# Spatial gating unit: mixing products placed between the z tiles, channel tiles finished one at a time, silu ahead of the slab halves

## The reference, cut to what matters

```python
def sgu_branch(h, w_in, ln_g, ln_b, w_s, b_s, w_out):
    uv, z = jnp.split(h @ w_in, [2 * SGU_WIDTH], axis=-1)
    u, v = jnp.split(jax.nn.gelu(uv), 2, axis=-1)
    v = layernorm(v, ln_g, ln_b).reshape(bsz, L // SGU_CHUNK, SGU_CHUNK, SGU_GROUPS, SGU_GROUP_DIM)
    w = jnp.where(tril[None], w_s, 0.0)
    s = jnp.einsum('gts,bnsgc->bntgc', w, v) + b_s.T[:, :, None]
    return (u * s.reshape(bsz, L, SGU_WIDTH) * jax.nn.silu(z)) @ w_out
```

## Time and profile before

| | us |
|---|---|
| median of 3 runs | 2149.76 (2148.75 to 2155.48) |
| profiled execution, its own time | 2146.33 |
| span of its trace, first to last instruction | 2144.4 |
| busy in the span: PE / DVE / ACT / POOL | 1979.3 / 1328.9 / 856.7 / 465.2 |
| mean granted clock of PE | 0.972 |

### The profile page before, as it was taken

The page is one execution under the profiler, slowest core; times in us unless marked ns, Lnnn a source line. Parts: engine busy times, 40 slices in busy tenths (PEclk is TensorE's granted clock), DMA queues, the critical chain, the costliest instruction groups (busy, mean ns, idle before and its releaser), DMA issues.

```text
span 2144.4 us, 24860 instructions
## 1 busy us (share of the span) xinstructions
PE 1979.3 (92%) x9910; PEld 1555.9 (73%) x9910; DVE 1328.9 (62%) x1920; ACT 856.7 (40%) x1236; POOL 465.2 (22%) x393
## 2 busy tenths in 40 slices
PE   4999898999999999999998899989989999899986
PEld 3777776788567888768897776867777766578865
DVE  5998985726549235544566454677378477637474
ACT  3325656312278224422332343355352354434332
POOL 5871110404159403032400101011002010100001
PEclk9999999999999999999999999999999999999998
DMA  3334431234222534433556626211132210123211
GB/s 131 120 145 142 139 125 54 81 120 148 103 98 84 171 118 157 158 95 131 186 147 149 149 80 125 79 59 41 62 112 83 84 40 20 40 79 129 97 60 59
DMA packets 63747, 225.21 MB, mean 105 GB/s; under 512 B 14144, under 2 KB 31216, under 8 KB 43280
## 3 DMA queue, kind: packets, MB, share of 16 engines
q1 hardware_dynamic: 22896, 162.54, 21.2%
q0 software_dynamic: 19760, 45.83, 7.2%
q10 hardware_dynamic: 20976, 15.26, 3.3%
HBM read 208.72 MB, written 14.81 MB: 104 GB/s over the span
## 4 chain that ended last, share of the span: by engine, by line
PE 64%; DVE 11%; ACT 5%; issue 3%; ACTq 1%; DMA 0%; POOL 0%; DVEq 0%; POOLq 0%
PE bank L486 18%; PE bank L487 18%; PE bank L488 18%; PE bank L485 2%; DVE ring_low L448 2%; PE bank L3362 1%; ACT ring_high L443 1%; PE bank L3393 1%; ACTq L2537 1%; ACT swa_s L3254 1%; PE bank L2061 1%; PE bank L622 1%; DVE lru_x L1975 1%; DVE swa_s L3172 1%; PE bank L3378 1%
## 5 line engine op out<-in xcount | busy, mean ns | idle before, releaser
L486 PE MATMUL bank<-h_high,ring_high 128*128 128x512 f32 x1248 | 504.7, 404 | 37.2 <-DVE h_low L1454 12.1
L448 DVE TENSOR_TENSOR ring_low<-ring,ring_high 128x2048 fp32r<-128x2048 f32 x136 | 326.5, 2401 | 316.4 <-ACT ring_high L443 316.1
L487 PE MATMUL bank<-h_low,ring_high 128*128 128x512 f32 x1248 | 491.9, 394 | 0.0
L488 PE MATMUL bank<-h_high,ring_low 128*128 128x512 f32 x1248 | 491.2, 394 | 0.0
L443 ACT ACTIVATE ring_high<-ring 128x2048 fp32r<-128x2048 f32 x145 | 277.4, 1913 | 475.1 <-PE bank L488 472.4
L486 PEld LDWEIGHTS bank<-h_high,ring_high 128*128 128x128 f32 x1248 | 238.1, 191 | 104.3 <-issue 35.7
L487 PEld LDWEIGHTS bank<-h_low,ring_high 128*128 128x128 f32 x1248 | 238.2, 191 | 52.8 <-issue 4.4
L488 PEld LDWEIGHTS bank<-h_high,ring_low 128*128 128x128 f32 x1248 | 238.0, 191 | 51.1
L448 POOL TENSOR_TENSOR ring_low<-ring,ring_high 128x2048 fp32r<-128x2048 f32 x9 | 44.1, 4904 | 375.6 <-ACT ring_high L443 375.6
L486 PE MATMUL bank<-gated_high,ring_high 128*128 128x512 f32 x256 | 104.8, 409 | 8.2 <-DVE sq L3658 5.0
L487 PE MATMUL bank<-gated_low,ring_high 128*128 128x512 f32 x256 | 102.6, 401 | 0.0
(11 more groups left out here) (520 smaller groups left out, 3833.8 us busy)
## 6 DMA issues: line engine op xcount, KB each, us to landing
ring<-slabs SPq DMA_DIRECT2D x149, 1024.0 KB, 4.8
acs_rows<-acs_rows POOLq DMA_DIRECT2D x16, 512.0 KB, 5.3
s_outputs<-s_ca POOLq DMA_DIRECT2D x4, 1152.0 KB, 5.0
x<-xT SPq DMA_DIRECT2D x2, 2048.0 KB, 8.7
exp_acs<-acs_rows POOLq DMA_DIRECT2D x16, 256.0 KB, 9.6
s_b<-s_br POOLq DMA_DIRECT2D x8, 512.0 KB, 4.6
s_rows<-s_powers POOLq DMA_DIRECT2D x16, 256.0 KB, 6.5
s_inputs<-s_w POOLq DMA_DIRECT2D x8, 512.0 KB, 3.0
```

Source lines behind the costliest of these rows:

```text
L448: dve.tensor_tensor(self.ring_low[:, s % RING, :], self.ring[:, s % RING, :], self.ring_high[:, self.splits_before[s] % AHEAD, :].bitcast( ...
L486: pe.matmul(out, w[0], x[0], start=start, stop=False)
L487: pe.matmul(out, w[0], x[1], start=False, stop=False)
L488: return pe.matmul(out, w[1], x[0], start=False, stop=stop)
```

## The change

A table `mixed` says which channel tiles' mixing goes behind which z tile: 0 behind z tile 4, 1 and 2 behind 5, 3 and 4 behind 6, and 5 to 7 behind 7. On PE the mixing products of those channel tiles stand right behind the z tile's products. On DVE the bias, the product with u and the gated low half of the tile before are in a function `mix(j)`, called behind the same z tiles; the low half of a slab moves behind `times_root` and `factor(i - 1)`, and the mask moves from i = 4 to i = 3, behind V's last token tile. On ACT silu of a tile comes ahead of the slab's high half, and the gated high halves are spread likewise. No instruction's size changes.

```diff
+    mixed = {4: (0,), 5: (1, 2), 6: (3, 4), 7: (5, 6, 7)}
...
         @block.scalar
...
             for i, (u, _) in enumerate(tiles):
-                C.split_high(act, u)
                 C.read(act, u)
                 act.activation(L.Z[:, i, :], L.Z[:, i, :], ACT.Silu).then_inc(gate.curve.sem, 1)
-            for j in range(KD):
-                gate.high_on_act(act, j)
+                C.split_high(act, u)
+                for j in mixed.get(i, ()):
+                    gate.high_on_act(act, j)
...
         @block.vector
...
-                if i == TC:
+                if i == TC - 1:
                     dve.tensor_tensor(L.W[:], L.W[:], C.mask[:].unsqueeze(1).to_broadcast([P, 16, P]), ALU.mult)\
                         .then_inc(wm.sem, 1)
-                C.split_low(dve, u)
                 C.full(dve, u)
                 times_root(dve, i, C.bank[u.b]).then_inc(C.bank_read[u.b], 1)
                 if i > 0:
                     factor(i - 1)
-            factor(KD - 1)
-            for j, u in enumerate(banks):
+                C.split_low(dve, u)
+                for j in mixed.get(i, ()):
+                    if j == KD - 1:
+                        factor(j)
+                    mix(j)
...
         @block.tensor
...
-            for t in tiles:
+            for i, t in enumerate(tiles):
                 C.gemm(pe, t, C.H.tiles(KD), seen)
-            pe.wait_ge(wm.sem, wm.at(0))
-            for j, u in enumerate(banks):
-                C.open(pe, u)
-                for n in range(TC):
+                for j in mixed.get(i, ()):
+                    u = banks[j]
+                    C.open(pe, u)
                     if j == 0:
-                        pe.wait_ge(vn.sem, vn.at(n))
+                        pe.wait_ge(wm.sem, wm.at(0))
+                        pe.wait_ge(vn.sem, vn.at(TC - 1))
```

More of the change, by code:

```diff
@@ L3625, in factor, with mix @@
                 dve.tensor_tensor(L.U[:, i, :], L.U[:, i, :], L.Z[:, i, :], ALU.mult).then_inc(gate.factor.sem, 1)
+            def mix(j):
+                u = banks[j]
+                C.full(dve, u)
+                v = lambda ap: ap.rearrange("p (n t) -> p n t", n=TC)
+                b = L.BS[:, j, :].unsqueeze(1).to_broadcast([P, TC, P])
+                s = C.sq[:, j % 4, :]
+                if j >= 4:
+                    dve.wait_ge(gate.mul.sem, gate.mul.at(j - 4))
+                dve.tensor_tensor(v(s), v(C.bank[u.b][:]), b, ALU.add).then_inc(C.bank_read[u.b], 1)
+                C.read(dve, u)
+                dve.wait_ge(gate.factor.sem, gate.factor.at(j))
+                dve.tensor_tensor(L.U[:, j, :], L.U[:, j, :], s, ALU.mult).then_inc(gate.mul.sem, 1)
+                if j > 0:
+                    gate.low_on_dve(dve, j - 1)
             for t in range(TC):
@@ L3668, in _ @@
             seen = set()
-            for t in tiles:
+            for i, t in enumerate(tiles):
                 C.gemm(pe, t, C.H.tiles(KD), seen)
-            pe.wait_ge(wm.sem, wm.at(0))
-            for j, u in enumerate(banks):
-                C.open(pe, u)
-                for n in range(TC):
+                for j in mixed.get(i, ()):
+                    u = banks[j]
+                    C.open(pe, u)
                     if j == 0:
-                        pe.wait_ge(vn.sem, vn.at(n))
[L3677 to L3681, removed]
+                        pe.wait_ge(wm.sem, wm.at(0))
+                        pe.wait_ge(vn.sem, vn.at(TC - 1))
+                    for n in range(TC):
+                        for e in range(2):
+                            g = 2 * j + e
+                            mm = pe.matmul(C.bank[u.b][64 * e:64 * e + 64, n * P:(n + 1) * P], L.V[:, n, g * 64:g * 64 + 64],
+                                           L.W[:, g, :], start=True, stop=True)
+                    mm.then_inc(C.bank_full[u.b], 1)
 def branch_sgu(C, last):
```

## The result

| | us |
|---|---|
| before, median of 12 runs | 2149.45 (2146.08 to 2155.48) |
| after, median of 12 runs | 2153.41 (2150.53 to 2157.75) |
| ratio after / before | 1.0018, 95% interval 1.0010 to 1.0025 |
| profiled execution of after: its span, clock | 2151.6, 0.972 |

The change costs 4.0 us (0.18%), with an interval that excludes zero. The two spans differ by more, 7.2 us, so I cut them at two marks: V's first normalising instruction, and the first product of the output projection.

What follows compares the result with a forecast made beforehand. The prediction took DVE's steps up to channel tile 6's bias addition as the bound. Waits of +3.8 plus clock and late tiles of +1.0 gave +4.8 us, so 2154.5 on the median of 2149.76, range 2149 to 2160.

Steps and rivals of the forecast that it cites:

- Bound: The output's first product waits for DVE's bias addition of channel tile 6, ending 2076.70, 0.36 us ahead of PE.
- the walk along DVE's steps: DVE's steps timed one by one to channel tile 6's addition, ending 2080.35 against 2076.70 before: +3.65 us.
- Two new waits: DVE waits 2.0 us for ACT's high half also behind z tiles 1 and 3: +4.0 us, less 0.2.
- Stall A: PE idle before z tile 4, whose slab's low half comes late: it starts 3.2 us later.
- Stall B: PE idle before mixing tile 0, between z tiles 4 and 5, waiting for the masked weights: 4.4 us.
- The clock and late tiles: Half clock after PE's idle stretches brings DVE z tile 5 late (+0.7) and tile 7 late (+0.3): together +1.0 us.
- The row of steps: DVE's steps ahead of channel tile 6's addition stay the same before and after; only waits change.
- PE becomes the bound: Rival: half clock through mixing tile 0 and z tile 5 (10.9 us) on PE; +9.4 us, 2159.2, chance 0.20.
- No cost: Rival: ACT's order costs DVE nothing, PE still waits for the mask; about +0.5 us, 2150.3, chance 0.13.
- a gain: Rival: mixing fills DVE's two earlier waits and the output starts at full clock; -6.0 us, 2143.8, chance 0.05.

Runs made afterwards that it cites:

- The square: Four variants of the changed kernel, between the marks: mixing 0 behind z tile 5, slab order before 49.00, changed 52.98 us; behind tile 4, 53.68 and 54.43.
- The run with neither cost: Changed kernel with slab halves in the order of before and channel tile 0's mixing behind z tile 5: 49.00 us between the marks, ratio 1.0001.
- the rearranged kernel: Changed kernel with mask in the stage ahead, high half ahead of silu, last slab's halves at the end, mixing from z tile 5: 2138.97 us, ratio 0.9946.

## Why the prediction was right, and where not

**Bound.** Right for the end, and too short. After the change too the bias addition of channel tile 6 releases the output's first product, 0.35 us ahead of it. But the earlier trace rows begin one row too late: ahead of ACT's high half stands the last product of z tile 7 (2058.63, shown above). DVE's row of steps alone set the end only from there. That PE's tile 7 came last before the change shows in the rows too: that wait was 2.10 us where the others are 1.9, and ACT started 0.19 us after its silu had ended (2058.17 plus 0.53). The margin was so small that the walk along DVE's steps gave nearly the same times, and so this slip did not spoil the forecast.

**Two new waits, +4.0 less 0.2.** Right in place and size: four waits of 1.90 where 2.0 were forecast and 1.91 and 2.10 stood before. The square gives 3.98 for the order, with the stall on the mask taken out. With the stall in, the waits behind tiles 3 and 5 are no longer on the chain, which goes from the mask on DVE over PE's mixing and z tiles 5 to 7.

**Stall A, 3.2.** Measured 3.13. **Stall B, 4.4 at full clock, 2.8 with tile 4 at half clock** (the mask at 2049.65 less 2046.9). Measured 2.55, with low clock behind A. That is under the 3 to 4.4 which the prediction gave as its sign, and its own figure with the low clock was under it as well.

**The clock and late tiles, +1.0.** Right in kind, short in size. DVE waits 0.57 for tile 5 and 0.72 for tile 7, and taking stall B away gave back 1.45. Tile 5 was expected at +0.7 and tile 7 at +0.3.

**The row of steps.** One slip, the other way. The prediction has the steps ahead of channel tile 6's addition the same before and after, and the walk put factor 7 ahead of channel tile 5's addition. In the changed code it stands behind the addition of channel tile 6 (the row at 2085.57 behind the one at 2083.64). Before, it stood ahead of all mixing on DVE:

```profile
2063.65 1.48 DVE L3625 TENSOR_TENSOR sgu_u<-sgu_u,sgu_z 128x512 f32<-128x512 f32 x2
```

These are factors 6 and 7. They took 1.39 us until the next instruction (2065.04) and not 1.20, because factor 7 waited for silu of tile 7. So 0.79 us leave the path, for which the prediction has no term. The run with neither cost shows it: 49.00 against 49.99, of which 0.79 is the factor and 0.21 the shorter last wait.

**Sum.** Forecast +4.8. Counted on DVE's rows: 3.59 more waiting for ACT, 1.29 for PE, 0.79 less for the factor, and 0.32 because an instruction with a wait behind it takes its full 0.68 and not the 0.60 after which the next one starts otherwise (four times more than before). That is +4.41, the stretch is +4.44, and the runs' medians differ by +3.96. The end of the span takes 0.43 back, nearly all of it (0.40) in the first nine products of the output, where the low clock ends sooner than before; I had called that 1.5 either way. On the median I forecast 2154.5, between 2149 and 2160, and it is 2153.4. That it came so near is partly luck: the late tiles were 0.45 short and the factor of 0.79 had no term, and the two go opposite ways.

**The rivals.** *PE becomes the bound* did not come about at its size: tile 5 at half clock took from 2053.98 until DVE had it at 2061.20, 7.2 us, and not 10.9. The low clock ended within it (0.74 in 2056 to 2058, 1.00 after). But its mechanism is nearer than its number says: the chain does run over PE from the mask to tile 7, and with ACT's order undone DVE waits 3.85 and 1.97 for PE. *No cost* would need both costs away (49.00); its sum has a slip, since 2077.5 less 2076.7 is +0.8 and not +0.5. The reason that I gave against a gain, that the mixing stands behind the low halves in DVE's order and fills no wait, fits the rows: all four waits stayed. In the rearranged kernel channels 0 and 1 stand ahead of the low half, and it waits for nothing.

**What the prediction had wrong underneath.** Its +1.0 is what the late tiles add on top of a DVE that is already late, and as such it is right in kind. What it does not see is that the stall alone would cost nearly as much as the whole change. Had I been asked what the change costs without its new order, I would have said +1.8 (that is the expectation on record) and it was +3.7. The step that I left out is that the high half behind a z tile needs the end of that tile on PE, so whatever delays PE comes to DVE by way of ACT. The same tie is why moving the mask alone gave nothing, where a row of steps on DVE alone would give 2.2.

The Trainium skill's rule that I weighed against the change ("TensorE: Matmul & The Clock Gate", "HAM oscillation — how this bites in real kernels") is borne out here in the main: the products behind both stalls soon stand at 0.50, and the one kernel in which the output starts after only 1.45 us of idle time starts it at 1.00. The rule has each burst start at the low clock. That is so behind the longer stall of 5.32 us (0.50 in the window from 2050, with the mixing products at 1.97 us), while behind those of 2.55 and 3.13 us the first products still had the high one (0.91 and 0.85).

## What to carry to other kernels

Before a producer's instruction is put behind a neighbour on an in-order engine, look whether that neighbour waits for the consumer: silu ahead of the slab half made ACT wait for DVE and DVE for ACT, four times 1.9 us, and no engine was busier. Interleaved work pays only where its own inputs are ready. A single wait (here for the mask, needed two steps later) stops all that queues behind it. Follow the chain of waits up past the engine that one has in mind, since the row ahead of it may be another engine's. And a term that is taken off one engine's row is worth something only up to the next tie to another engine, so follow each wait to what really releases it before summing. Here the gain lay in moving what nobody needed yet (the last slab's halves), 4.1 us for a few lines.

## What the runs showed of the hardware

- Low clock came behind shorter gaps than I had looked at in the trace before, and not at once: 2.55 us of idle time (with a tile at partly half clock ahead of it) was followed by 0.91, 0.50 and 0.74 in windows of 2 us, and 3.13 us by 0.85, 0.50 and 0.80. Gaps of 1.14 us (ahead of z tile 4, with only ACT's order undone) and of 1.45 us were not followed by it.
- Behind longer gaps it came at once and stayed longer: behind 5.32 us of idle time the granted clock was 0.50 in all three windows from 2050 to 2056 and 0.90 in the next.
- The hand-over through ACT and DVE is steady within 0.02 us: the wait for a slab half behind silu is 1.89 to 1.91 in all seventeen cases in which nothing but silu and the high half came between (four each after the change, with the slab order alone and with channel 0 later, and five in the other kernels).
